# Second block's attention scores: own keys on partitions 0 to 63, context keys on 64 to 127, queries on both

## The reference, cut to what matters

```python
# window attention: 8 query heads, 2 key heads, blocks of 128 queries
s_win = einsum(qb, kb) * scale          # own keys: the block, the one before, the one behind; banded
s_ctx = einsum(qb, kc) * scale          # 256 context keys
p = softmax(concatenate([s_win, s_ctx, s_sink]))
# neighbourhood attention: 4 heads
s_nb  = einsum(qr, kr) * scale + bias   # all 512 own keys, masked by columns
s_ctx = einsum(qr, kc) * scale
p = softmax(concatenate([s_nb, s_ctx]))
# layer 0 alone: the context tokens attend to the context keys (context_gqa, context_mha)
```

## Time and profile before

| | |
|---|---|
| median of 3 runs | 2872.91 us (2870.44 to 2874.6) |
| profiled execution, its own time | 2878.19 us |
| its span in the trace | 2876.4 us |
| PE, DVE, ACT busy | 2628.1, 1089.8, 708.5 us |
| the six score phases of the second block, first product to last | 321.8 us |
| of these, PE busy | 292.04 us |

### The profile page before, as it was taken

How to read it: one execution, slowest core, us unless ns; L and a number is a source line. 1 busy time by engine, 2 the same in 40 slices (tenths; PEclk the granted TensorE clock), 3 DMA queues, 4 the chain that set the end, 5 groups by cost and what they waited for, 6 DMA issues and landing times. The chain is left out here.

```text
span 2876.4 us, 43155 instructions
## 1 busy us (share of the span) xinstructions
PE 2628.1 (91%) x17316; PEld 1391.2 (48%) x17316; DVE 1089.8 (38%) x2320; ACT 708.5 (25%) x1851; POOL 219.5 (8%) x256
## 2 busy tenths in 40 slices
PE   7999999999998899998799999987899969999987
PEld 3565654664645666655344444435566543332222
DVE  3022340213345665457322121236652562333224
ACT  2134321333322245332111111113342321000000
POOL 1100200000101001012000000001100010000000
PEclk9999999999999999998899999998999979999999
DMA  7244615442614001115899999972102239999996
GB/s 224 82 128 106 166 55 139 110 132 78 158 50 118 6 1 43 66 47 212 321 392 395 401 401 395 400 216 54 28 1 95 96 143 358 410 406 410 411 410 262
DMA packets 268621, 569.96 MB, mean 198 GB/s; under 512 B 12416, under 2 KB 203200, under 8 KB 219328
## 3 DMA queue, kind: packets, MB, share of 16 engines
q1 hardware_dynamic: 256512, 528.69, 50.3%
q0 software_dynamic: 11824, 39.18, 5.0%
q10 hardware_dynamic: 144, 0.14, 0.0%
HBM read 551.53 MB, written 16.42 MB: 197 GB/s over the span
## 5 line engine op out<-in xcount | busy, mean ns | idle before, releaser
L460 PE MATMUL ps<-turned,ring 128*128 128x512 f32 (+1 forms) x1408 | 551.3, 552 | 10.2 <-ACT turned L1594 8.8
L460 PEld LDWEIGHTS ps<-turned,ring 128*128 128x128 f32 x1408 | 270.6, 193 | 279.6 <-issue 259.0
L705 PE MATMUL ps<-ring,mixT 128*128 128x512 f32 x512 | 224.1, 597 | 0.8 <-DVE mixT L1775 0.8
L1249 ACT ACTIVATE work<-ps 128x512 f32<-128x512 f32 x32 | 19.1, 598 | 684.5 <-PE ps L1153 404.3
L506 PE MATMUL ps<-kz,qz 96*128 96x256 f32 (+3 forms) x384 | 165.6, 519 | 24.0 <-DVE qz L2197 8.8
L705 PEld LDWEIGHTS ps<-ring,mixT 128*128 128x128 f32 x512 | 97.0, 191 | 118.7 <-issue 117.3
L1816 ACT ACTIVATE probsT<-ps 128x512 f32<-128x512 f32 (+3 forms) x280 | 120.2, 455 | 136.4 <-PE ps L546 106.7
L1803 ACT ACTIVATE probs_v<-ps,col 128x256 f32<-128x256 f32 (+5 forms) x216 | 136.4, 632 | 70.2 <-DVE col L1753 35.0
L1749 DVE TENSOR_REDUCE col<-ps 128x1 f32<-128x256 f32 (+4 forms) x136 | 78.8, 579 | 176.0 <-PE ps L506 169.6
L471 PE MATMUL ps<-ring,turned 128*128 128x128 f32 x1216 | 140.3, 278 | 4.5 <-ACT turned L1594 4.5
L532 PE MATMUL ps<-const,probs_v 128*128 128x128 f32 x752 | 125.6, 284 | 20.2 <-DVE probs_v L1767 18.1
(11 more groups left out here) (299 smaller groups left out, 3575.4 us busy)
## 6 DMA issues: line engine op xcount, KB each, us to landing
ring<-in_w_gate SPq DMA_DIRECT2D x64, 1024.0 KB, 20.0
mixT<-in_w_up SPq DMA_DIRECT2D x64, 1024.0 KB, 13.9
ring<-in_w_mod SPq DMA_DIRECT2D x96, 512.0 KB, 4.0
ring<-in_w_up SPq DMA_DIRECT2D x48, 1024.0 KB
ring<-in_w_in SPq DMA_DIRECT2D x82, 512.0 KB, 7.3
turned<-in_w_gate SPq DMA_DIRECT2D x32, 1024.0 KB
mixcT<-in_w_down SPq DMA_DIRECT2D x32, 1024.0 KB
probs_v<-in_w_down SPq DMA_DIRECT2D x32, 1024.0 KB
```

The source lines that it names most:

```text
L460: mm = nc.tensor.matmul(ps[:, b, 0:n], w[:, k, :], rhs[:, k, 0:n], start=(k == 0), stop=(k == KD - 1))
L705: mm = nc.tensor.matmul(ps[:, b, :], lhs[:, k, tl * P:(tl + 1) * P], w, start=(k == 0), stop=(k == KD - 1))
```

## The change

The context keys move to partitions 64 to 127 of `KC`, the own keys stay on 0 to 63, and the queries lie on both halves. A unit's two products then take 64 rows each, of different halves; the context product of `wa` becomes one of 256 columns and stands ahead of the masks. A wide unit's PSUM span is moved so that the context scores begin at a bank's edge, and a unit now waits by whole banks. The copies of the queries: `wa` gets a new ACT instruction per pair of heads (`act_queries_twice`, 64 partitions by 1024 columns) and PE waits for that one; `nb` evacuates its queries twice; the context's queries go to the upper half alone. GpSimd no longer clears rows 64 to 95.

```diff
         def score_span(u):
 
             o = (seq[u] % 2) * 1024 if wide(u[0]) else (seq[u] % 4) * 512
+            if wide(u[0]):
+
+                o += SEQ - (keys_of(u) - NC) * P
             return o, o + keys_of(u) * P
+
+        def score_banks(u):
+
+            o, end = score_span(u)
+            return o // 512 * 512, -(-end // 512) * 512
...
-            w = before(u, score_span)
+            w = before(u, score_banks)
...
-            q = (QC if kind in ("ca", "cb") else qz)[0:KROWS, hh, t * P:(t + 1) * P]
+            q = qz[0:KROWS, hh, t * P:(t + 1) * P]
+            own, other = slice(0, HD), slice(HD, P)
...
             elif kind in ("ca", "cb"):
-                parts = [(q, KC[0:KROWS, part if kind == "ca" else 2 + hh, :], 0)]
+                parts = [(QC[other, hh, t * P:(t + 1) * P], KC[other, part if kind == "ca" else 2 + hh, :], 0)]
             elif kind == "nb":
-                parts = [(q, kz[0:KROWS, hh, :], 0), (q, KC[0:KROWS, 2 + hh, :], SEQ)]
+                parts = [(qz[own, hh, t * P:(t + 1) * P], kz[own, hh, :], 0),
+                         (qz[other, hh, t * P:(t + 1) * P], KC[other, 2 + hh, :], SEQ)]
             else:
...
-                parts = [(q, kz[0:KROWS, part, j0 * P:(j1 + 1) * P], 0)]
+                parts = [(qz[own, hh, t * P:(t + 1) * P], kz[own, part, j0 * P:(j1 + 1) * P], 0),
+                         (qz[other, hh, t * P:(t + 1) * P], KC[other, part, :], w)]
                 if t > 0:
                     parts.append((unit16, before16, 0))
                 if t < NT - 1:
 
                     parts.append((unit16, causal16, w - P))
-                parts += [(q, KC[0:KROWS, part, c * P:(c + 1) * P], w + c * P) for c in range(NC)]
...
-                pe.wait_ge(*at("roped", (l, "aq", 2 * part + 1)))
-                pe.wait_ge(*at("zero_rows", ("second", l)))
+                pe.wait_ge(*at("queries_twice", (l, 2 * part + 1)))
...
-            for e in range(2):
-                ins = nc.scalar.activation(dst[0:HD, 2 * (c % 2) + e, 0:n], ps[e * HD:(e + 1) * HD, bank_of(job), 0:n],
-                                           ACT.Copy, scale=scale)
+            for half in {"bq0": (0, 1), "aq1": (1,), "bq1": (1,)}.get(f"{name}{r}", (0,)):
+                for e in range(2):
+                    ins = nc.scalar.activation(dst[half * HD:(half + 1) * HD, 2 * (c % 2) + e, 0:n],
+                                               ps[e * HD:(e + 1) * HD, bank_of(job), 0:n], ACT.Copy, scale=scale)
...
+        def act_queries_twice(act, l, c):
+
+            act.wait_ge(*at("roped", (l, "aq", c)))
+            o = 2 * (c % 2)
+            nc.scalar.activation(qz[HD:P, o:o + 2, :], qz[0:HD, o:o + 2, :], ACT.Copy).then_inc(*done("queries_twice", (l, c)))
...
+            act_queries_twice(act, l, 0)
             for part in range(2):
...
                 if part == 0 or l == 0:
                     roots_table()
+                if part == 1:
+                    act_queries_twice(act, l, 2)
+                act_queries_twice(act, l, 2 * part + 1)
                 act_softmax(act, ("wa", l, part))
...
-                ins = nc.scalar.activation(KC[0:HD, first + e, :], ps[e * HD:(e + 1) * HD, bank_of(job), 0:CTX], ACT.Copy)
+                ins = nc.scalar.activation(KC[HD:P, first + e, :], ps[e * HD:(e + 1) * HD, bank_of(job), 0:CTX], ACT.Copy)
...
-                nc.gpsimd.memset(QC[HR, :, :], 0.0)
-                nc.gpsimd.memset(KC[HR, :, :], 0.0)
-                nc.gpsimd.memset(qz[HR, :, :], 0.0)
-                nc.gpsimd.memset(kz[HR, :, :], 0.0).then_inc(*done("zero_rows", ("second", l)))
```

More of the change, by code:

```diff
@@ L2528, in _ @@
                     pool.wait_ge(sem("bias_landed"), 32 * (HEADS * l + hh + 1))
-                    pool.wait_ge(*at("zero_rows", ("second", l)))
                     rows14 = b[:, 64:960].rearrange("p (s k) -> p s k", k=64)
```

## The result

| | before | after |
|---|---|---|
| median, same chip | 2871.76 us (4 runs, 2870.44 to 2874.6) | 2914.17 us (4 runs, 2910.8 to 2921.03) |
| ratio | | 1.0134, 95% interval 1.0114 to 1.0155 |
| profiled execution | 2878.19 us | 2921.03 us |
| six score phases | 321.8 us | 310.3 us |

What follows compares the result with a forecast made beforehand. It took PE to bound most `wa` phases, DVE layer 0 part 0, and a loop over two engines `nb`. Gains in the phases less shape changes and later starts summed to -3.6 us from 2872.91, giving 2869.3, range 2862 to 2880.

Steps and rivals of the forecast that it cites:

- The rest of the program keeps its instructions: Outside the six score phases: nothing changes, so a microsecond won or lost in a phase passes to the end.
- four `wa` phases with `ca` (steady, openings, shape changes): Window phases: steady pairs -6.0 us, openings -3.9; new shape changes in `ca` and `cb` units cost +1.6 together.
- two `nb` phases: Neighbourhood phases: the loop goes through one unit's scores per pair, hiding 0.43 us each; 3.6 a phase, -7.2 in all.
- layer 0: later starts of part 0, part 1: Window phases of layer 0: ACT's query copies delay PE's start, +1.3 us; part 1, with a slower-clock opening, +5.7.
- layer 1: later starts of part 0, part 1, `nb`: Layer 1: query copies delay the window phases by +2.4 and +1.3 us, four evacuations instead of two delay `nb` by +1.2.
- Overlap: Score units: products on different row halves run together, hiding the shorter one, 0.50 us in `wa`, 0.43 in `nb`.
- the forecast's 1.00 and 0.60: Steady `wa` pair: 0.50 us hidden in each unit, less shape-change and other deductions, leaving 0.40 of 5.05 won.
- the 0.05 that the forecast takes off in each unit: Steady `wa` units: last deduction in 0.50 - 0.15 - 0.05 = 0.30 and 0.50 - 0.15 - 0.20 - 0.05 = 0.10 us.
- The rival that charged the drain alone: Shape changes: each costs only the array wait, 0.10 us; a pair wins 0.65, -7.4 in all, 2865.5; chance 0.05.
- the clock rival: Phase openings: later starts lengthen half clock, up to 2 us each for four more phases, +4.4, 2877; chance 0.15.
- The copies: Second query copies: ACT's 64x1024 copy takes 1.1 us, plus 0.15 for a hand-over, delaying the starts of phases.
- No overlap: Score units: products of unequal widths or these operands do not overlap, leaving only costs; +23 us, 2896; chance 0.07.

Runs made afterwards that it cites:

- e1: Kernel after with 128 long-fulfilled waits in PE's program ahead of layer 0's expert loop; 2870.9 us, ratio 0.9989 to the kernel before.
- e2: Kernel before, without the change, with 128 such waits on PE ahead of layer 0's expert loop; 2922.61 us, ratio 1.0165.
- e8: Kernel before with one joined context product of 256 columns ahead of the masks, 96 rows kept, and 128 waits; 2874.27 us, ratio 1.0000.
- e5: Kernel after with 128 waits, both products on the lower half (64 rows), no second copy of queries; 2916.19 us, ratio 1.0143.
- e7: Kernel after with 128 waits, DVE writing the window queries' rotation sum to both halves, no ACT copies; 2867.73 us, ratio 0.9972.
- e11: Kernel after with 96 waits, DVE writing the window queries' rotation sum to both halves, no ACT copies; 2864.23 us, ratio 0.9959.
- e4: Kernel after with 32 waits on PE ahead of layer 0's expert loop; 2921.29 us (one run).

## Why the prediction was wrong

It said 2869 us and the kernel took 2914. The step that failed stands in the first paragraph: "The rest of the program keeps its instructions." It lets only time won or lost in the phases pass to the end, and puts nothing for the code behind them. The instructions were kept, their place was not. The 128 that the change removes ahead of layer 0's loop move its about 1,614 by half a page. By the arithmetic of pages they then touch eight; by count each turn fetches nine packets and stalls PE, 43.0 us in five turns. No rival had it. e1 and e2 show it from both sides: +43 us for a shift of 128, with the change or without. With the loop in place the same change gives 0.9989 (0.9976 to 1.0003), where the forecast of -3.6 us is 0.9987; no gain at all lies in that interval too. So the runs neither confirm nor refute the sum, and its terms erred both ways. Term by term, in the kernel after against before:

| term | forecast | measured |
|---|---|---|
| four `wa` phases with `ca` (steady, openings, shape changes) | -9.9, and part of +1.6 | -0.8 - 2.4 - 5.3 - 4.1 = -12.6 |
| two `nb` phases | -7.2, and part of +1.6 | -1.1 + 2.2 = +1.1 |
| layer 0: later starts of part 0, part 1 | +1.3, +5.7 | 1.5, 5.6 |
| layer 1: later starts of part 0, part 1, `nb` | +2.4, +1.3, +1.2 | 3.0, 1.1, 1.2 |
| sum | -3.6 | +0.9 |

*Overlap: right.* Own and context product of unequal widths begin 0.01 us apart (time line of PE, `nb` of layer 1):

```profile
2254.40 1.19 PE L516 MATMUL ps<-kz,qz 64*128 64x512 f32 x1 [2.69 <-ACT qz L1846]
2254.41 0.79 PE L516 MATMUL ps<-work,qz 64*128 64x256 f32 x1
```

The pair of `wa` has 4.62 us, where 4.65 was forecast, against 5.05 (time line of PE, layer 1, part 1):

```profile
2187.00 0.72 PE L542 MATMUL ps<-const,probs_v 128*128 128x128 f32 x5
2187.81 0.59 PE L516 MATMUL ps<-kz,qz 64*128 64x384 f32 x1
2187.81 0.70 PE L516 MATMUL ps<-work,qz 64*128 64x256 f32 x2
2188.23 0.48 PE L516 MATMUL ps<-kz,qz 64*128 64x384 f32 x1
2188.65 0.28 PE L516 MATMUL ps<-masks 128*128 128x128 bf16 x2
...
2192.43 0.59 PE L516 MATMUL ps<-kz,qz 64*128 64x384 f32 x1
```

e8 and e5 take this apart: -0.10 for the joined product, +0.38 for 64 rows and their changes of shape, -0.71 for the overlap. In the last, the two products now take 0.84 us to the masks where e5 has 1.28, so 0.88 is hidden in a pair, and 0.17 comes back between the transposes and the scores (0.81 in place of 0.64). With the joined product's 0.10 that is 0.98 won and 0.55 lost, near the forecast's 1.00 and 0.60; the 0.05 that the forecast takes off in each unit has no row behind it. The Trainium skill, "TensorEngine Tiling (Array Packing)", section Key Properties, has TensorE drain at each change of tiling mode. The rival that charged the drain alone would have won 0.65 a pair, and the trace has 0.43.

*`nb`: mechanism and size right while the clock is up; the clock was underpriced.* The chain that ended last shows the forecast loop, scores 1.08 instead of 1.50 and 5.92 us from scores to scores instead of 6.33:

```profile
2277.79 1.08 PE ps L516 x2
...
2278.90 0.71 DVE ps L1754
...
2282.24 1.46 PE ps L556 x24
2283.71 1.08 PE ps L516 x2
```

What took the gain back is the clock rival, at its own place: granted clock 0.92 and 0.83 in the `nb` phases against 0.97 and 0.97 before. e7 shows what the term is worth where the clock stays up: -3.1 and -4.6, with `cb`'s cost in the first and up to 1.7 of clock in the second (1.00 against 0.97). The forecast had -7.2 for both. From e7's -7.7 to the +1.1 of the kernel after are 8.8 us, and these two phases have 30 us at half clock there against 4 in e7. The prediction named this sign itself, a low clock for longer than 10 us behind a start; it had priced the rival at 4.4 in all.

*The copies: right.* ACT's copy of 64x1024 takes 1.05 us (forecast 1.1):

```profile
L2201 ACT ACTIVATE qz<-qz 64x1024 f32<-64x1024 f32 x8 | 8.3, 1052 | 5.3 <-DVE qz L2214 5.2
```

and layer 0's part 1 starts 5.4 us later on the time line. e7 shows that 4 us of it were the wait for ACT's queue (table load, silu, two copies): with the second copy on DVE the phase starts at 1077.36 instead of 1081.41.

*"No overlap" was priced far too low.* The rival had +23 us: 0.36 lost a pair, some 3 in the openings, 1.6 in the context units, and 13.2 of waits that e5, which makes no copies, does not have. e5 measures +41 all the same, though a pair loses less, 0.28 (5.33 against 5.05). The openings, priced at 3, had 71 us more at half clock than before, up to 35 us.

## What to carry to other kernels

Where an engine has a long hardware loop, count its instructions, and after any edit ahead of it look at the queue of instruction packets inside the loop: silence there is part of the tuning, and a row of idle waits restores it. A small edit that comes out some tens of microseconds slow should be tried once more with padding before its idea is judged. Splitting the rows of a product pays only where the halves really run together and the copies that it needs are cheap (e11: 0.4%); where they don't, the time lost by clock can be several times the time lost by shape changes (e5). A second copy of data should be made by the engine that makes the first, not by one whose queue stands ahead of the phase: that gave back 4 us at layer 0's part 1, and nothing at layer 1's part 0.

## What the runs showed of the hardware

- A backward branch over about 1,614 instructions of PE costs nothing in one place and 8.5 us in another, 64 instructions away (e4 and e11, shifts of 32 and 96): some 5.5 us of stall and the half clock behind it, with 9 packets of 16 KB a turn. The edge, between 33 and 77 by the arithmetic above, was not looked for. Nor was the number of pages that PE can hold measured by itself.
- The same products over 64 instead of 96 rows, the 32 being zeros, ran with 114 instead of 41 us at half clock in six phases (one trace each): zero rows were worth 42 us. Two products of 64 rows side by side (e1) have 58.
- A DVE copy of 64x1024 fp32 took 0.686 us, a sum of 64x512 0.685, an ACT copy of 64x1024 1.05.
